# A fused fp32 layer pair on one core: the entry and the sums of one merge stage re-ordered, and three smaller edits of waits and order

## The reference, cut to what matters

```
def branch_merge(attn, gla, gate_a, gate_g, w_br_attn, w_br_gla, w_out):
    y = sigmoid(gate_a) * (attn @ w_br_attn) + sigmoid(gate_g) * (gla @ w_br_gla)
    return y @ w_out
mod_x = split(silu(c) @ w_ada + b_ada, 6)      # shift, scale and gate vectors, six times 1024
```

## Time and profile before

| what | value |
|---|---|
| median of the runs | 1761.55 us |
| the profiled execution's own time | 1762.64 us |
| its span | 1760.8 us |
| PE, share of the span | 97% |
| DVE, ACT, POOL, share of the span | 58%, 48%, 40% |
| PE clock granted, mean of the span | 0.996 of full |

### The profile page before, as it was taken

How to read it: one execution, slowest core, us unless ns; L and a number is a source line. 1 busy time by engine, 2 the same in 40 slices (tenths; PEclk the granted TensorE clock), 3 DMA queues, 4 the chain that set the end, 5 groups by cost and what they waited for, 6 DMA issues and landing times.

```text
span 1760.8 us, 24655 instructions
## 1 busy us (share of the span) xinstructions
PE 1702.6 (97%) x8729; PEld 1384.4 (79%) x8729; DVE 1019.3 (58%) x1600; ACT 842.5 (48%) x1472; POOL 705.5 (40%) x795
## 2 busy tenths in 40 slices
PE   9999999979999999999989999999999999999998
PEld 6877777756786667878878888888888888888887
DVE  6677685678457864376658657766624443232322
ACT  5465665876366654356542354465523332323131
POOL 2634445415442015311124423234245555555554
PEclk9999999999999999999999999999999999999999
DMA  7362624322321003201048521111133323333333
GB/s 221 109 198 77 189 74 121 97 71 72 86 88 39 25 13 87 60 25 37 25 152 257 177 61 37 49 48 49 48 96 96 96 73 99 97 103 96 96 96 108
DMA packets 217151, 160.55 MB, mean 91 GB/s; under 512 B 8334, under 2 KB 190615, under 8 KB 217047
## 3 DMA queue, kind: packets, MB, share of 16 engines
q1 hardware_dynamic: 201758, 125.50, 24.8%
q10 hardware_dynamic: 15288, 33.66, 5.8%
HBM read 156.98 MB, written 2.16 MB: 90 GB/s over the span
## 4 chain that ended last, share of the span: by engine, by line
PE 64%; issue 12%; DVE 9%; ACT 8%; POOL 7%; DMA 1%; POOLq 0%; DVEq 0%; ACTq 0%; SPq 0%
PE ps L658 14%; PE ps L662 14%; PE ps L659 13%; POOL wl L608 7%; PE ps L3147 3%; PE ps L3150 3%; PE ps L3148 3%; PE ps L2206 2%; PE ps L2188 1%; ACT wh L621 1%; PE ps L1653 1%; PE ps L1621 1%; PE ps L2195 1%; PE ps L2711 1%; PE ps L2745 1%
## 5 line engine op out<-in xcount | busy, mean ns | idle before, releaser
L608 POOL TENSOR_TENSOR wl<-raw,wh 128x256 fp32r<-128x256 f32 (+1 forms) x775 | 682.1, 910 | 995.7 <-ACT wh L621 995.7
L658 PE MATMUL ps<-ah,wh 128*128 128x512 f32 (+1 forms) x1144 | 458.1, 400 | 12.5 <-ACT gate_u L2784 4.2
L662 PE MATMUL ps<-ah,wl 128*128 128x512 f32 (+1 forms) x1144 | 447.3, 391 | 0.2
L659 PE MATMUL ps<-al,wh 128*128 128x512 f32 (+1 forms) x1144 | 446.5, 390 | 0.0
L621 ACT ACTIVATE wh<-raw 128x1024 fp32r<-128x1024 f32 (+1 forms) x220 | 230.7, 1049 | 300.9 <-PE ps L662 155.4
L658 PEld LDWEIGHTS ps<-ah,wh 128*128 128x128 f32 (+1 forms) x1144 | 213.9, 187 | 67.6 <-ACT wh L621 9.8
L662 PEld LDWEIGHTS ps<-ah,wl 128*128 128x128 f32 (+1 forms) x1144 | 213.9, 187 | 49.5 <-POOL wl L608 1.9
L659 PEld LDWEIGHTS ps<-al,wh 128*128 128x128 f32 (+1 forms) x1144 | 214.1, 187 | 43.8 <-issue 1.7
L658 PE MATMUL ps<-bh,wh 128*128 128x512 f32 (+1 forms) x332 | 134.7, 406 | 9.6 <-DVE resid L1478 3.6
L662 PE MATMUL ps<-bh,wl 128*128 128x512 f32 (+1 forms) x332 | 131.1, 395 | 0.8 <-POOL wl L608 0.7
L659 PE MATMUL ps<-bl,wh 128*128 128x512 f32 (+1 forms) x332 | 130.5, 393 | 0.0
(11 more groups left out here) (451 smaller groups left out, 2966.6 us busy)
## 6 DMA issues: line engine op xcount, KB each, us to landing
raw<-w_mlp SPq DMA_DIRECT2D x64, 512.0 KB, 3.9
raw<-w_in SPq DMA_DIRECT2D x52, 512.0 KB, 3.8
raw<-ssm_w_in SPq DMA_DIRECT2D x40, 512.0 KB, 3.9
ada_late<-w_ada ACTq DMA_DIRECT2D x16, 1024.0 KB, 6.5
ada_raw<-w_ada ACTq DMA_DIRECT2D x16, 512.0 KB, 4.5
cum_rows<-cum_saved ACTq DMA_DIRECT2D x16, 512.0 KB, 3.9
raw<-ssm_w_out SPq DMA_DIRECT2D x16, 512.0 KB, 3.4
raw<-mla_w_in SPq DMA_DIRECT2D x11, 512.0 KB, 4.0
```

The costliest lines, as they stand in the source:

```text
L608: nc.gpsimd.tensor_tensor(wl[:, s, part], raw[:, s, part], wh[:, s, part].bitcast(F32), ALU.subtract).then_inc(lo_ready, LOW_PIECES * (par ...
L658: nc.tensor.matmul(dst, w_hi[k], x_hi[k], start=k == 0, stop=False)
L659: nc.tensor.matmul(dst, w_hi[k], x_lo[k], start=False, stop=False)
L662: ins = nc.tensor.matmul(dst, w_lo[k], x_hi[k], start=False, stop=k == n - 1)
```

## The change

- MLA scores: the one wait for all exponentials of the head before is replaced by one wait ahead of each tile's scores, for the exponentials of the bank that the tile is written to.
- Grouped attention, DVE: in the third step of a head `low_q` of the next head stands ahead of `scale`.
- ACT: the high part of the gate's weights of round 1 is copied ahead of the high part of head 7, and no longer behind the sigmoid of round 0.
- PE: the branch projection of round 0 goes to bank 3 and waits chunk by chunk for the low parts of the heads, and no longer for all of them and bank 1 at its start.
- DVE: in round 0 the product stands ahead of the modulation of block 0.
- PE: the sums of block i-2, and no longer of block i-1, stand at the end of round i; blocks 6 and 7 are summed at the end of the stage.

```
@@ scores(h) of the MLA heads
-                if h:
-                    pe.wait_ge(sem("exp_done"), h * TT)
-                else:
+                if h == 0:
                     pe.wait_ge(sem("padded"), 2)
                 for t in range(TT):
+                    if h and t:
+                        pe.wait_ge(sem("exp_done"), (h - 1) * TT + t + 1)
+                    elif h:
+                        pe.wait_ge(sem("exp_done"), (h - 1) * TT + 2)
@@ act_gqa
+            split_ahead(act, "branch_a", 0, 0)
             high(QH - 1)
@@ dve_gqa, steps
                     top(n + 1)
+                if t == 2 and j + 1 < QH:
+                    low_q(j + 1)
                 if n + 1 < NQ:
                     scale(n + 1)
...
-                if t == 2 and j + 1 < QH:
-                    low_q(j + 1)
@@ pe_branch
+        ENTRY_BANK = 3
...
                     unit_ready(pe, name, i, n)
+                    if name == "branch_a" and i == 0:
+                        head_low = lambda k: pe.wait_ge(acc_free[1], ACC0["gqa"][1] + 2 + k + 1)
+                        project(bank(ENTRY_BANK), name, n, chunk(bh), chunk(bl), DC, P, before=head_low).then_inc(unit_done, 1)
+                        continue
...
                 if name == "branch_a":
-                    for block in range(LATE_DONE[i - 1] if i else 0, LATE_DONE[i]):
+                    for block in range(LATE_DONE[i - 2] if i > 1 else 0, LATE_DONE[i - 1] if i else 0):
                         late_sums(block)
             if name == "branch_a":
-                for block in range(LATE_DONE[DC - 1], LATE_BLOCKS):
+                for block in range(LATE_DONE[DC - 2], LATE_BLOCKS):
                     late_sums(block)
@@ act_branch
-                split_ahead(act, name, i, 0)
+                if name == "branch_g" or i:
+                    split_ahead(act, name, i, 0)
@@ dve_branch
-                if first:
+                if first and i:
                     for m in range(late, late + LATE_STEPS[i]):
                         modulate_late(m)
                     late += LATE_STEPS[i]
...
-                    nc.vector.tensor_tensor(merged[:, i], bank(1), branch_gate[:], ALU.mult).then_inc(acc_free[1], 1)
+                    nc.vector.tensor_tensor(merged[:, i], bank(1 if i else ENTRY_BANK), branch_gate[:], ALU.mult).then_inc(acc_free[1], 1)
...
                     dve.sem_inc(taken, 1)
+                    if i == 0:
+                        for m in range(LATE_STEPS[0]):
+                            modulate_late(m)
+                        late += LATE_STEPS[0]
```

## The result

The changed kernel takes 1794.49 us (median of 4 runs, 1793.93 to 1795.68) against 1761.46 us before (four runs too) on the same chip: a ratio of 1.018, 95% interval 1.0166 to 1.0194. It is slower, by 1.8%. The profiled execution of after took 1794.3 us against 1762.64, 31.7 us more; the forecast was 28.9 more. The order of reading is that of before: first the busy shares, then PE's waits, then the stage.

The account below looks back on a forecast made before the run. PE, busy 97%, was taken as the bound, with the second `mod_late` buffer the stage's limit. 1762.64 + 32.0 (stage) - 2.1 (query low parts) - 1.0 (score waits) = 1791.5, less part of 1.1: 1791 us, range 1779 to 1801.

Parts of the forecast that it names:

- The buffer is the limit, a round moved is a round lost: Branch stage: later sums hold `mod_late`'s second buffer, so product follows modulation; rounds 16.8 us against 11.83, stage costs 32.0.
- 8.96 us from the sums to PE's restart: Each round: 0.14 us to the modulation, 7.99 to its product's start behind it, 0.83 to PE.
- The clock, 1.5 us a round: PE's work after each 3.5 us idle runs partly at the lower clock, losing 1.5 us; ends 0 and 3.0.
- The entry: Start of branch stage: branch 1 starts 5.5 us earlier, but PE waits 4.2 us in round 2; gain 2.3 us.
- S(2): End of PE's sums in round 2: forecast at 937.4, against 939.65 before.
- The exit: End of stage: last modulation leaves PE idle 8.2 us, then 0.8 of sums and 1.5 of clock before GLA.
- Score waits, -1.0: MLA scores: at most 1.9 us of waits saved, part returning at transposes; -1.0 us, bounds -1.9 and +4.5.
- Query low parts, -2.1: Grouped attention: `low_q` hides in DVE's 1.06 us idle, both `q_lo` waits go; -2.1 us, bounds 0 and -2.1.
- The second rival: Seven idle stretches: the clock does not fall, -10.5 us, 1781; ground: waits of 1.5 us and below show none; 13%.

Follow-up runs that it names:

- e9: Changed kernel with unused products on PE, 14 ahead of the branch projections of rounds 2 to 7 and 28 ahead of the last sums: 1781.2 us, ratio 1.0103.
- e5: Kernel before with only the score waits per bank: ratio 0.9998.
- e6: Kernel before with only `low_q` moved ahead of `scale`: 1759.77 us, ratio 0.9979.
- e11: The changed kernel itself, run again unaltered on another chip, against the kernel before: 1794.46 us, ratio 1.0176.
- e10: Changed kernel with half of the modulation's work left out, 2 of 4 operations per call: 1765.59 us, ratio 1.0012.

## Why the prediction was right, point by point

- *The buffer is the limit, a round moved is a round lost.* Right, and shown from four sides: the shift alone brings the loss, the sums put back remove it, a third buffer removes it with the sums left late, and half the modulation shrinks it as the sum says.
- *8.96 us from the sums to PE's restart.* The trace has 0.10 + 8.05 + 0.84 = 8.99 (934.38 to 943.37). One POOL subtraction fell into each modulation, as forecast.
- *The clock, 1.5 us a round.* Near. From the restart to the sums it took 7.34 us, 1.8 more than the 5.5 of a projection in dense work, but not all of that is the clock: at the full clock, in e9, a projection behind a short wait took 5.77 us (941.40 to 947.17). So the clock has 7.34 - 5.77 = 1.57 us (1.67 by whole rounds, 17.13 - 15.46), and 0.3 us is the restart itself, which my sum put at nothing. The rounds so are 17.13 instead of 16.76 us, 1.9 us in all over five.
- *The entry.* PE ended its attention at 900.41 (903.36 before) and S(2) was 934.38; the forecast, less its 3.1 us of earlier gains, was 934.3. Two small errors cancel in it. The first `ada_late` took 5.4 us from issue to DVE's start against 5.3 before, where I had added 0.5, so the product came 0.3 us earlier. And the projection behind it took 1.9 us more than 5.5, where I had 1.5. PE's wait in round 2 was 3.5 and not 4.2 us also because its gate ended 0.4 us later than forecast: the wait for `wl`, which I had said would go, was still 0.2 us there (it was 0.8).
- *The exit.* The idle was 6.6 us and not 8.2, for two reasons. I had left the sums of block 6 (0.8 us, PE at work) out of it, and this modulation took 7.28 us and not 7.99. POOL's subtraction comes there in four short pieces, and the operations beside them took 1.04 to 1.10 us each. But the clock and the restart took back more: the last sums 1.89 us instead of 0.8 (1.07 in e9 at the full clock), and GLA's start is 29.7 us late while its first copy of a result (1037.37 against 1005.67) is 31.7 us late, 2 us lost in between. I had 1.5 for both; it was 3.1.
- *Score waits, -1.0.* The stage from its first scores to its last outputs took 114.7 instead of 115.3 us, -0.6. The direction of the doubt was right: most of the 1.9 us came back, and e5 can't be told from no change. PE's waits for `probs_t` grew from 4.3 to 7.7 us in all.
- *Query low parts, -2.1.* 146.1 instead of 148.7 us, -2.6 in the trace of after, and -1.9 in e6, -2.5 without its lower clock. The division was not delayed: DVE still idled 0.46 us ahead of it (1.06 before).

```profile
879.40 0.68 DVE L2406 TENSOR_TENSOR q_lo<-p_cos,q_hi 128x512 fp32r<-128x512 f32 x1
880.55 0.16 DVE L2436 RECIPROCAL g_rinv<-g_rsum 128x1 f32<-128x1 f32 x1 [0.46 <-ACT g_probs L2298]
```

- *The second rival's ground,* that waits of 1.5 us and below show no lower clock, doesn't hold in the trace of before. Near 1113 us PE waited 0.5 and 1.2 us with one short product between, and then ran mostly at the lower level (timeline of PE and a stretch, both of before). The rival's condition did not come true in the rounds: the clock fell in each of the six, in after as in e11, whose waits are the same.

```profile
1113.13 0.47 PE L658 MATMUL ps<-ah,wh 128*128 128x512 f32 x1 [1.23 <-ACT gate_u L2784]
```

```profile
1114.00:1118.00 4.00, 4.00 (x13) 3.11 (x11) 2.76 (x3) 0.30 (x1) 3.35 (x4) 0.57 0.00 0
```

So the steps held. The 2.8 us that are missing in the sum are 1.9 in the rounds, most of it the restart, and 1.6 of clock and restart at the exit, less the 0.7 by which the last modulation was shorter. The Trainium skill's rule (TensorE: Matmul & The Clock Gate, HAM oscillation) takes half of the time at the low rate as the penalty; for the (1 - 0.79) x 2 x 8 = 3.4 us of after's stretch that is 1.7 us a round. The runs agree with it within 0.1 us (1.57 to 1.67).

## What to carry to other kernels

With two buffers, ask of each release not only whether its consumer can wait, but what the producer's queue does behind its own wait: here a sum that was not needed before the next stages held a buffer, and behind that wait stood a product that PE needed at once. Where work on a side engine comes in blocks between products that the main engine needs, compute how late a product may come (here one gate less the hand-over, 4.5 us) and deal out the blocks below that. Gains at the entry of a chain count only up to its next fixed point.

## What the runs showed of the hardware that was not expected

- After an idle of 6.6 us PE's clock was low for longer than after the 3.4 us ones: 1.2 GHz through the last sums and on to about 4 us into GLA's work, against some 3.4 us after a wait in a round. In a round the fall also came late: the first five matmuls of the projection from 943.37 us on still came about 0.23 us apart, and only then seven 0.43 us apart.
- Filling the idle with unused products (3.2 us in each of the 3.4 us waits, 6.4 us in that of 6.6) kept the granted clock at 1.00 in the stage and made the kernel 13.3 us faster (e9).
- At the full clock too a projection costs more behind a wait than in dense work: 5.77 us (e9) against 24 x 0.227 = 5.45.
- Like waits were not always followed by a like clock. Behind a wait of 2.81 us the kernel before had 0.66 over 919 to 924 us; behind one of 2.83 us e10 had 1.00 over 924 to 929 us and over 929 to 934. Behind the wait of 1.6 us for the first probabilities, near 760 us, the kernel before had 1.00 over 755 to 765 us and e6 0.83.
- POOL's subtraction of 128x1024 in one piece stretched one DVE operation from 0.75 to 2.84 us; in four pieces of 128x256 it stretched three to 1.10 and one to 1.04, 1.3 us together instead of 2.1.
